# Which engine adds the second row of a pair: by tile, or by what stands beside the pair

## The chip, the cores and the metric

The kernel runs on one core of a Trainium2 chip. The metric is the device time of one execution in microseconds (us). A core has TensorE (PE in the profile; its weight loads are PEld), VectorE (DVE), ScalarE (ACT), GpSimd (POOL) and SyncE (SP), each with its own queue of instructions, and 16 DMA engines. Here SP issues the ordinary transfers and GpSimd the gathers by index.

## What is computed

One layer of a hybrid encoder for 1024 prompt tokens and 64 sample tokens, with 1024 values each. The first half, here called the front, is a normalization, a projection to 3608 columns, three mixers (a gated linear attention, an attention with forgetting, a cross-attention into 256 memory tokens), a gated mix of their outputs and an output projection. The second half is a retrieval of experts, of which there are 16,384. It is this half that the change touches:

```python
def one_block(xb):                       # 128 tokens
    q = (xb @ w_q).reshape(blk, PEER_HEADS, 2, PEER_DHALF)
    s = jnp.einsum('thpc,hpkc->thpk', q, sub_keys, ...)
    ...                                  # the best 16 experts of a token and head: idx, softmax weights g
    u = jnp.take(u_tab, idx, axis=0)
    a = jax.nn.gelu(jnp.einsum('thkd,td->thk', u, xb, ...), approximate=False)
    w = (g * a).astype(xb.dtype)
    return jnp.einsum('thk,thkd->td', w, jnp.take(v_tab, idx, axis=0))
```

For each token, 8 heads choose 16 experts each. An expert is one row u and one row v of 1024 values; in the kernel the two lie side by side in one row of 8 KB. The output is the sum of the rows v, each weighted by its softmax weight times the gelu of the dot product of u and the token.

## The kernel before

**Tiles and groups.** The 1088 tokens are 9 tiles of 128 (the last has 64). The front works on groups of tiles: tile 0, tiles 1 and 2, tiles 3 to 5, tiles 6 to 8. While the experts of one group's tiles are worked through, the front of the next group runs beside them; the first group's front runs alone, and beside the last group's experts nothing runs.

**Pairs.** The experts are worked through in pairs: for tile i, head r and number q, two expert rows for each of the 128 tokens, 8 pairs for a head and 64 for a tile, 544 in all (the last tile packs its 64 tokens twice and has 32). GpSimd gathers the two rows into two of the 8 slots of `c_ring` (L1847, 128 rows of 8 KB for each). VectorE forms the two dot products (L1768, each a long instruction and a short one that reads the accumulator into `l_dots`). ScalarE takes the gelu (L1448), multiplies with the softmax weights (L1451) and scales a unit matrix with the result (L1456, into `l_diag`). TensorE multiplies this diagonal with the v half of the slot and adds into `c_p_y` in PSUM, two matmuls of 512 columns for a row (L1284; in the trace each of them is two records). The second row can instead be added by VectorE in SBUF: `l_ysb` = row times weight + `l_ysb` (L1784), and then its diagonal isn't built. At a tile's end `finish` adds `c_p_y` and `l_ysb` (L1795). A slot is gathered into again when the pair that used it is done: GpSimd waits for TensorE (`s_vdone`) and, where VectorE adds the second row, for `s_vapart` too. It runs three pairs ahead of VectorE.

**Who adds the second row.** `apart(n)` says for pair n whether VectorE does. Before, it does so for all tiles of the first three groups (384 pairs); for the last group's 160 pairs TensorE adds both rows.

**The order.** `make_plan` writes one list of steps: after each pair stand the steps of the next group's front that belong beside it, spread by weights, and the last 16 pairs of a group have none. The steps are `in_prep` (normalization), `in_unit` (projection), `mix`, `fox` and `past` (the mixers), `gate` (gated mix), `out` (output projection) and `sco` (scores of the experts). Each engine walks this list. TensorE takes the steps beside a pair first and then the pair's matmuls. VectorE takes the pair's dot products, then the second row of the pair before (`values`), then a piece of the choice of experts for a later head (`pick`, L1710 to L1758), and then the steps. ScalarE takes the pair first too.

In the walk that follows, stretches of the trace are named by the front's steps beside which they run. For the last group that is 2254 to 2467 us for the projection, 2467 to 3010 for the mixers, 3010 to 3286 for the gated mix, 3396 to 3516 for the scores, 3516 to 3603 for the tail without steps; from 3603 us on the last group's experts run alone.

Of the kernel before, what the change touches and what calls it, by code (L numbers as in the profile page):

```python
# [74 lines left out]

def pair_index(i, r, q):
    return (i * HEADS + r) * 8 + q if i < TILES else TILES * HEADS * 8 + r * 4 + q


def apart(n):  # L80


    return ALL_PAIRS[n][0] < GROUPS[-1][0]


def apart_before(n):
    return sum(apart(k) for k in range(n))


ALL_PAIRS = [(i, r, q) for i in range(NT) for r in range(HEADS) for q in range(pairs_of(i))]  # L90
# [62 lines left out]
def make_plan():  # L153


    plan = [(None, [s]) for s, _ in front_steps(0)]
    plan.append((("start",), []))
    for g in range(len(GROUPS)):
        pairs = [("pair", i, r, q) for i in GROUPS[g] for r in range(HEADS) for q in range(pairs_of(i))]
        ahead = front_steps(g + 1) if g + 1 < len(GROUPS) else []  # L160
        total = sum(w for _, w in ahead)
        slots = len(pairs) - 2 * pairs_of(GROUPS[g][-1])
        done, k = 0.0, 0
        for n, pair in enumerate(pairs):
            beside = []
            while k < len(ahead) and done + ahead[k][1] / 2 <= total * (n + 1) / slots:
                beside.append(ahead[k][0])
                done += ahead[k][1]
                k += 1
            plan.append((pair, beside))  # L170
        assert k == len(ahead)
    plan.append((("end",), []))
    return plan


class Scope:
# [302 lines left out]
def layer(nc, c, t_in, outs, dram, ctx):  # L479

    m = Scope(nc, ctx, "l")
    sb, pb, sem = m.sb, m.pb, m.sem
    PLAN = make_plan()


    wa2, ba_bc, go_bc, bf_bc, gq_bc, gk_bc, gm_bc = c.wa2, c.ba_bc, c.go_bc, c.bf_bc, c.gq_bc, c.gk_bc, c.gm_bc
# [991 lines left out]
    def _(dve):  # L1478
# [294 lines left out]
        def values(n):  # L1773
# [1 line left out]
                return  # L1775
            i, r, q = ALL_PAIRS[n]
            T, j, col = width_of(i), (n * PAIR + 1) % RING, q * PAIR + 1
            if r == 0 and q == 0:
                dve.wait_ge(s_xres, 16 * (i + 1))
            if n:  # L1780
                dve.wait_ge(s_vapart, apart_before(n))
            dve.wait_ge(s_diag, n + 1)
            y = ysb[i % 2]
# [3 lines left out]
        def finish(i):  # L1787
            T = width_of(i)
            r, q = HEADS - 1, pairs_of(i) - 1
            dve.wait_ge(s_vdone, pair_index(i, r, q) + 1)  # L1790
            dve.wait_ge(s_xres, 16 * (i + 1))
            if apart(pair_index(i, r, q)):
                dve.wait_ge(s_vapart, apart_before(pair_index(i, r, q) + 1))
            y = ysb[i % 2]
            tt(out=y[:T, :], in0=p_y[:T, :], in1=y[:T, :], op=ALU.add).then_inc(s_yev, 1)  # L1795
# [150 lines left out]
```

## Time and profile before

| | |
|---|---|
| median of 3 runs | 4438.22 us (4433.03 to 4452.79) |
| profiled execution | 4445.82 us, span 4444.1 us |
| TensorE busy | 3389.7 us (76%) |
| VectorE busy | 2805.9 us (63%) |
| ScalarE busy | 1582.2 us (36%) |
| GpSimd busy | 1216.8 us (27%) |
| moved by DMA | 1484.95 MB, mean 334 GB/s |
| granted TensorE clock, mean | 0.875 of full speed |

The busy time of an engine is a sum over stretches that have different limits. The granted clock has two levels, 1.2 and 2.4 GHz; a mean of 0.75 in a stretch says that half of it passed at 1.2 GHz. TensorE's matmuls are pipelined and their ends are modelled, so its busy time overstates its work. Where the chain of waits names an instruction, that instruction ended last at that point; the same instruction elsewhere may cost nothing.

### The profile page before, as it was taken

Reading aid. Unit: us, or ns where it says so; the run is one execution under the profiler, and the core shown is the slowest. Engines: PE = TensorE matmul, PEld = TensorE weight load, DVE = VectorE, ACT = ScalarE, POOL = GpSimd, SP = SyncE. Lnnn points to the kernel's source line nnn. Section 1 sums busy time; section 2 is a strip of 40 time slices with the busy share of each in tenths; the row PEclk is TensorE's granted clock in tenths of the full one; section 3 lists DMA queues with packets and bytes.
Section 4 is the critical chain, followed back from the end, with each engine's and each line's share of the span. In section 5 each row is a group of like instructions: output and inputs, shape, how many; then the busy total and the mean of one; then the engine's idle time right before and its main releaser. Section 6 shows DMA issues by size and latency. Waiting matters only on the chain.

```text
span 4444.1 us, 33979 instructions
## 1 busy us (share of the span) xinstructions
PE 3389.7 (76%) x10219; PEld 1759.7 (40%) x10219; DVE 2805.9 (63%) x6048; ACT 1582.2 (36%) x3679; POOL 1216.8 (27%) x1122
## 2 busy tenths in 40 slices
PE   5765965986896776989689777576978867777777
PEld 4462444842444443544234344233543322322222
DVE  1112454547656784646777788685767886676677
ACT  1111154422315563432232455253443233333333
POOL 0000211113221222322333232242323344444443
PEclk9787976997997788999889778778989989999989
DMA  7557865889996788879999897878989999999998
GB/s 239 189 200 270 333 215 196 321 319 387 364 351 238 257 306 325 339 291 352 402 387 422 310 362 283 295 285 356 413 351 370 403 414 421 418 415 421 402 373 371
DMA packets 298492, 1484.95 MB, mean 334 GB/s; under 512 B 42740, under 2 KB 112372, under 8 KB 147716
## 3 DMA queue, kind: packets, MB, share of 16 engines
q0 software_dynamic: 156672, 1140.92, 64.7%
q1 hardware_dynamic: 141636, 341.86, 21.2%
q8 instruction: 81, 1.33, 0.1%
q14 instruction: 103, 0.84, 0.0%
HBM read 1415.59 MB, written 67.08 MB: 334 GB/s over the span
## 4 chain that ended last, share of the span: by engine, by line
PE 40%; DMA 24%; DVE 18%; ACT 6%; issue 6%; POOL 2%; SPq 1%; POOLq 0%; DVEq 0%; ACTq 0%
DMA c_ring<-in_uv,l_idx 17%; PE c_p_y L1284 11%; DVE c_ring L1768 7%; PE c_PB L1016 4%; PE c_PC L1016 4%; DVE l_ysb L1784 3%; PE c_PA L1271 2%; PE c_PA L1226 2%; PE c_PB L1271 2%; PE c_PB L1226 2%; PE c_PC L1226 2%; DMA c_area<-oT_sp 2%; POOL c_ring L1847 2%; PE c_PA L1254 1%; DMA c_area<-in_w_out 1%
## 5 line engine op out<-in xcount | busy, mean ns | idle before, releaser
L1847 POOL DMA_INDIRECT c_ring<-in_uv,l_idx x1088 | 1210.0, 1112 | 3203.8 <-PE c_p_y L1284 1400.0
L1284 PE MATMUL c_p_y<-c_ring,l_diag 128*128 128x512 f32 (+1 forms) x2816 | 1510.5, 676 | 451.5 <-ACT l_diag L1456 444.3
L1768 DVE CUSTOM_DVE_ANT_0 c_ring<-c_ring,l_h_cur 128x1024 f32<-128x1024 f32 x1088 | 1302.8, 1221 | 365.1 <-DMA c_ring<-in_uv,l_idx 356.6
L1284 PEld LDWEIGHTS c_p_y<-c_ring,l_diag 128*128 128x128 f32 (+1 forms) x2816 | 551.0, 207 | 1237.6 <-ACT l_diag L1456 650.9
L1448 ACT ACTIVATE l_gel<-l_dots 128x2 f32<-128x2 f32 x544 | 110.7, 203 | 1606.2 <-DVE l_dots L1768 1604.9
L1784 DVE SCALAR_TENSOR_TENSOR l_ysb<-c_ring,l_wgt,l_ysb 128x1024 f32<-128x1024 f32 x384 | 492.4, 1282 | 0.0
L1448 ACT ACT_TABLE_LOAD x207 | 265.6, 1283 | 60.0 <-DVE l_dots L1768 56.6
L1451 ACT ACTIVATE l_wgt<-l_gel,l_gw 128x1 f32<-128x1 f32 x1088 | 261.2, 287 | 17.9
L1456 ACT ACTIVATE l_diag<-c_ident,l_wgt 128x128 f32<-128x128 f32 x640 | 243.1, 399 | 16.7
L1016 PE MATMUL c_PB<-c_area 128*128 128x451 f32 (+1 forms) x576 | 228.4, 550 | 1.9 <-ACT c_area L1317 1.2
L1016 PE MATMUL c_PC<-c_area 128*128 128x451 f32 (+1 forms) x576 | 226.4, 546 | 4.3 <-DMA c_area<-in_w_in 4.3
L1226 PE MATMUL c_PA<-c_area 128*128 128x128 f32 (+3 forms) x512 | 132.1, 415 | 115.8 <-DMA c_area<-oT_sp 113.5
L1016 PEld LDWEIGHTS c_PB<-c_area 128*128 128x128 f32 (+1 forms) x576 | 107.1, 187 | 122.8 <-issue 119.0
L1226 PEld LDWEIGHTS c_PA<-c_area 128*128 128x128 f32 x512 | 93.5, 203 | 155.2 <-issue 126.0
L1016 PEld LDWEIGHTS c_PC<-c_area 128*128 128x128 f32 (+1 forms) x576 | 105.9, 185 | 123.7 <-issue 117.2
L1668 DVE TENSOR_TENSOR c_area<-c_area,c_PA 128x128 f32<-128x128 f32 (+3 forms) x32 | 14.0, 438 | 205.8 <-ACT c_area L1405 205.8
L1166 PE MATMUL c_PC<-c_ident,c_area 128*128 128x128 f32 (+2 forms) x328 | 66.4, 318 | 98.7 <-ACT c_area L1392 54.2
L1271 PE MATMUL c_PA<-c_area 128*128 128x512 f32 (+1 forms) x288 | 130.3, 607 | 1.9 <-ACT c_area L1414 1.9
L1271 PE MATMUL c_PB<-c_area 128*128 128x512 f32 (+1 forms) x288 | 128.3, 599 | 2.5 <-DMA c_area<-rw_sp 2.5
L1226 PE MATMUL c_PB<-c_area 128*128 128x128 f32 (+3 forms) x512 | 123.8, 395 | 0.0
L1226 PE MATMUL c_PC<-c_area 128*128 128x128 f32 (+3 forms) x512 | 122.9, 393 | 0.0
L1254 PE MATMUL c_PA<-c_area 128*128 128x512 f32 (+1 forms) x192 | 91.3, 632 | 24.9 <-DMA c_area<-in_w_out 21.8
(284 smaller groups left out, 3679.4 us busy)
## 6 DMA issues: line engine op xcount, KB each, us to landing
c_area<-in_w_gb SPq DMA_DIRECT2D x32, 2304.0 KB, 10.0
c_area<-in_w_in SPq DMA_DIRECT2D x32, 1804.0 KB, 9.2
c_area<-rw_sp SPq DMA_DIRECT2D x16, 2048.0 KB, 10.8
c_ring<-in_uv,l_idx POOLq DMA_INDIRECT x1088, 10.1
c_area<-in_w_out SPq DMA_DIRECT2D x8, 2048.0 KB, 9.7
proj<-c_area SPq DMA_DIRECT2D x64, 225.5 KB, 7.1
c_area<-proj SPq DMA_DIRECT2D x8, 1288.0 KB, 6.0
c_ring<-in_w_qT SPq DMA_DIRECT2D x16, 512.0 KB, 7.6
```

The costliest lines, as they stand in the source:

```text
L1016: ins = mm_(banks[2 + u % 4][:T, :PW], hT_in[:, dt, j * 128:j * 128 + T], w[:, dt * PW:(dt + 1) * PW], start=dt == 0, stop=dt == DT - 1)
L1166: ins = tr_(PC[:widths[b], (b % 4) * 128:(b % 4) * 128 + T], prob[h % 2][:T, b * 128:b * 128 + widths[b]], c.ident[:T, :T])
L1226: mm_(ps[:, 0:N], w[:, at:at + 128], g_hT[:, e, 0:N], start=e == 0, stop=e == DT - 1)
L1254: ins = mm_((PA, PB)[j % 2][:T, half * 512:(half + 1) * 512], mixT[:, dt, j * 128:j * 128 + T], w[:, dt * 512:(dt + 1) * 512], start=dt == ...
L1271: ins = mm_(banks[v % 4][:T, :], hT_out[:, dt, j * 128:j * 128 + T], w[:, dt * 512:(dt + 1) * 512], start=dt == 0, stop=dt == DT - 1)
L1284: ins = mm_(p_y[:T, e * 512:(e + 1) * 512], diag[:, j, :T], ring[:, j, D + e * 512:D + (e + 1) * 512], start=r == 0 and q == 0 and k == 0, ...
L1448: a_(gel[:, c0:c0 + PAIR], dots[:, c0:c0 + PAIR], ACT.Gelu).then_inc(s_ae, 1)
L1451: ins = nc.scalar.mul(wgt[:, c0 + k:c0 + k + 1], gel[:, c0 + k:c0 + k + 1], gw[:, head % 3, c0 + k:c0 + k + 1])
L1456: ins = nc.scalar.mul(diag[:, (n * PAIR + k) % RING, :T], unit[:, :T], wgt[:, c0 + k:c0 + k + 1])
L1768: ins = nc.vector.tensor_tensor_reduce(out=ring[:, j, 0:D], in0=ring[:, j, 0:D], in1=h_cur[i % 2][:, :], scale=1.0, scalar=0.0, op0=ALU.mu ...
L1784: nc.vector.scalar_tensor_tensor(out=y[:T, :], in0=ring[:T, j, D:2 * D], scalar=wgt[:T, col:col + 1], in1=y[:T, :], op0=ALU.mult, op1=ALU. ...
L1847: nc.gpsimd.indirect_dma_start(out=ring[:, j, :], out_offset=None, in_=t_in["uv"][:, :], in_offset=bass.IndirectOffsetOnAxis(ap=idx[:, hea ...
```

## The change

Whether VectorE adds a pair's second row no longer goes by the pair's tile but by what stands beside the pair in the plan: it does so where one of the steps is `in_unit`, `gate`, `out` or `sco`. Beside mixer steps alone, beside `in_prep` alone, and where no step stands, TensorE adds both rows. For this the plan is made once, ahead of the functions that ask. `values` and `finish` count the rows that VectorE has added so far instead of taking every pair before.

```diff
-def apart(n):
-    return ALL_PAIRS[n][0] < GROUPS[-1][0]
-
-def apart_before(n):
-    return sum(apart(k) for k in range(n))
...
+PLAN = make_plan()
+
+def sums_apart():
+    return [any(step[0] in ("in_unit", "gate", "out", "sco") for step in beside)
+            for expert, beside in PLAN if expert and expert[0] == "pair"]
+
+APART = sums_apart()
+
+def apart(n):
+    return APART[n]
+
+def apart_before(n):
+    return sum(APART[:n])
...
-            if r == 0 and q == 0:
-                dve.wait_ge(s_xres, 16 * (i + 1))
-            if n:
+            dve.wait_ge(s_xres, 16 * (i + 1))
+            if apart_before(n):
                 dve.wait_ge(s_vapart, apart_before(n))
...
-            if apart(pair_index(i, r, q)):
+            if apart_before(pair_index(i, r, q) + 1):
                 dve.wait_ge(s_vapart, apart_before(pair_index(i, r, q) + 1))
```

By the plan 168 pairs keep their second row on VectorE. The 216 others are these:

| the front of group | beside mixers | no step, scattered | no step, tail | `in_prep` |
|---|---|---|---|---|
| tiles 1, 2 | 12 | 0 | 16 | 1 |
| tiles 3 to 5 | 36 | 8 (6 in the gated mix, 1 in the output projection, 1 in the scores) | 16 | 2 |
| tiles 6 to 8 | 67 | 39 (11 in the projection, 1 after the mixers, 14 in the gated mix, 5 in the output projection, 8 in the scores) | 16 | 3 |

Three places show what moves. The line numbers after the change are 10 higher. First VectorE before, beside the forgetting attention of tile 7, two pairs with the steps behind them (L1648 copies transposed probabilities, L1641 and L1642 mask scores and take their maximum):

```order
L1768 ISA c_ring,l_dots<-c_ring,l_h_cur 128x1024
L1768 ISA l_dots 128x1
L1768 ISA c_ring,l_dots<-c_ring,l_h_cur 128x1024
L1768 ISA l_dots 128x1
L1784 SCALAR_TENSOR_TENSOR l_ysb<-c_ring,l_wgt,l_ysb 128x1024
L1641 TENSOR_TENSOR c_PB<-c_PB,c_causal 128x128
L1642 TENSOR_REDUCE l_fmax<-c_PB 128x1
L1648 COPY c_area<-c_PC 128x384
```

And the same place on VectorE after the change:

```order
L1778 ISA c_ring,l_dots<-c_ring,l_h_cur 128x1024
L1778 ISA l_dots 128x1
L1778 ISA c_ring,l_dots<-c_ring,l_h_cur 128x1024
L1778 ISA l_dots 128x1
L1651 TENSOR_TENSOR c_PB<-c_PB,c_causal 128x128
L1652 TENSOR_REDUCE l_fmax<-c_PB 128x1
L1658 COPY c_area<-c_PC 128x384
```

The addition into `l_ysb` is gone from between the dot products and the mixer's steps; nothing else moved. TensorE before, in the same attention (L1166 transposes probabilities, L1148 to L1151 form scores, L1179 multiplies with the values):

```order
L1166 MATMUL c_PC<-c_ident,c_area 128x128 x4
L1148 MATMUL c_PB<-c_area 128x512
L1150 MATMUL c_PB<-c_area 128x256
L1151 MATMUL c_PB<-c_area 128x128
L1166 MATMUL c_PC<-c_ident,c_area 128x128 x3
L1179 MATMUL c_PC<-l_V,c_area 128x64 x7
L1284 MATMUL c_p_y<-c_ring,l_diag 128x512 x2
```

And TensorE there after the change:

```order
L1176 MATMUL c_PC<-c_ident,c_area 128x128 x4
L1158 MATMUL c_PB<-c_area 128x512
L1160 MATMUL c_PB<-c_area 128x256
L1161 MATMUL c_PB<-c_area 128x128
L1176 MATMUL c_PC<-c_ident,c_area 128x128 x3
L1189 MATMUL c_PC<-l_V,c_area 128x64 x7
L1294 MATMUL c_p_y<-c_ring,l_diag 128x512 x4
```

The pair's matmuls have become four, at the same point, ahead of the next step's transposes. Last, TensorE before in the projection of the last group (L1016), where every third pair or so has no step:

```order
L1016 MATMUL c_PB<-c_area 128x451 x8
L1284 MATMUL c_p_y<-c_ring,l_diag 128x512 x4
L1016 MATMUL c_PB<-c_area 128x451 x8
L1284 MATMUL c_p_y<-c_ring,l_diag 128x512 x2
L1016 MATMUL c_PC<-c_area 64x451 x8
```

And TensorE there after the change:

```order
L1026 MATMUL c_PB<-c_area 128x451 x8
L1294 MATMUL c_p_y<-c_ring,l_diag 128x512 x6
L1026 MATMUL c_PB<-c_area 128x451 x8
L1294 MATMUL c_p_y<-c_ring,l_diag 128x512 x2
L1026 MATMUL c_PC<-c_area 64x451 x8
```

Where a pair with a step and one without follow each other, four matmuls have become six: the pair without a step brings two more between two units of the projection.

## Rows read from the trace of the kernel before

**Rows 1.** The page: busy time, and the chain that ended last, by engine

```profile
PE 3389.7 (76%) x10219; PEld 1759.7 (40%) x10219; DVE 2805.9 (63%) x6048; ACT 1582.2 (36%) x3679; POOL 1216.8 (27%) x1122
...
PE 40%; DMA 24%; DVE 18%; ACT 6%; issue 6%; POOL 2%; SPq 1%; POOLq 0%; DVEq 0%; ACTq 0%
```

**Rows 2.** Windows by stretch; the first row names the columns

```profile
core 0: us, PE busy (x) PEld busy (x) DVE busy (x) ACT busy (x) POOL busy (x), PEclk, DMA share, GB/s
...
572.00:727.00 155.00, 106.51 (x478) 76.26 (x478) 98.01 (x211) 88.50 (x178) 23.29 (x23) 0.72 0.52 181
...
1017.00:1118.00 101.00, 61.69 (x100) 21.72 (x99) 75.38 (x155) 23.79 (x73) 36.32 (x32) 0.76 0.98 389
...
1321.00:1665.00 344.00, 251.34 (x1052) 159.29 (x1051) 255.71 (x546) 203.93 (x386) 72.08 (x73) 0.77 0.73 268
1665.00:1935.00 270.00, 235.47 (x689) 131.06 (x688) 161.37 (x328) 111.88 (x205) 71.06 (x61) 0.94 0.85 329
...
2254.00:2467.00 213.00, 206.99 (x505) 89.50 (x504) 168.22 (x336) 56.46 (x171) 79.84 (x70) 0.97 1.01 415
2467.00:3010.00 543.00, 372.96 (x1359) 207.46 (x1358) 417.65 (x879) 263.06 (x541) 160.92 (x137) 0.75 0.83 305
...
3396.00:3516.00 120.00, 115.54 (x260) 46.35 (x259) 92.42 (x180) 30.81 (x94) 45.62 (x40) 0.98 0.99 397
3516.00:3603.00 87.00, 49.44 (x76) 16.14 (x75) 75.28 (x154) 23.30 (x72) 37.76 (x32) 0.80 1.00 404
3603.00:4264.00 661.00, 487.22 (x1022) 189.78 (x1023) 461.57 (x1126) 226.82 (x709) 275.94 (x259) 0.97 1.01 416
```

**Rows 3.** Windows of the forgetting attention: tile 5, then tiles 6, 7, 8

```profile
1590.00:1665.00 75.00, 64.51 (x313) 42.23 (x314) 66.49 (x139) 52.82 (x99) 18.54 (x19) 0.86 0.81 300
2541.00:2631.00 90.00, 72.96 (x296) 44.95 (x295) 81.75 (x165) 51.20 (x101) 28.91 (x28) 0.83 0.96 358
2691.00:2782.00 91.00, 73.30 (x274) 43.66 (x273) 80.08 (x154) 54.93 (x102) 26.75 (x24) 0.81 0.76 275
2892.00:2985.00 93.00, 72.15 (x234) 33.21 (x235) 79.85 (x176) 53.49 (x110) 38.72 (x25) 0.73 0.75 281
```

**Rows 4.** The chain by line in the three mixer stretches, 572:727, 1321:1665, 2467:3010

```profile
by line: DVE c_ring L1768 11.4%; PE c_p_y L1284 5.7%; issue 4.9%; PE c_PC L1166 4.7%; ACT L1392 4.1%; ACT c_area L1392 3.6%; PE c_PC L1099 3.2%; DVE l_ysb L1784 3.1%; ACT c_area L1358 2.5%; PE c_PA L1059 2.5%; PE c_PC L1068 2.4%; PE c_PA L1
...
by line: DVE c_ring L1768 11.9%; issue 8.7%; PE c_p_y L1284 6.9%; DMA c_ring<-in_uv,l_idx 6.1%; DVE l_ysb L1784 5.6%; PE c_PC L1166 3.4%; PE c_PC L1179 3.2%; DMA l_V<-proj 3.1%; PE c_PC L1099 2.0%; PE c_PB L1148 2.0%; ACT c_area L1358 1.7%;
...
by line: DVE c_ring L1768 17.2%; issue 9.6%; DVE l_ysb L1784 8.9%; PE c_p_y L1284 5.5%; DMA c_ring<-in_uv,l_idx 3.5%; DMA l_V<-proj 2.7%; DMA c_area<-in_fox_logf 2.1%; DMA oT_sp<-c_area 2.0%; PE c_PB L1148 1.8%; PE c_PC L1068 1.5%; DMA kT_s
```

**Rows 5.** The chain by line in 2254:2467, 3396:3516, 1665:1935, 3010:3286

```profile
by line: DMA c_ring<-in_uv,l_idx 28.0%; PE c_PB L1016 23.4%; PE c_p_y L1284 17.3%; PE c_PC L1016 11.7%; issue 5.2%; DVE l_ysb L1784 3.4%; DVE c_ring L1768 3.2%; POOL c_ring L1847 2.9%; DVE c_area L1515 0.6%; DVE l_pos L1732 0.5%; ACT l_wgt 
...
by line: DMA c_ring<-in_uv,l_idx 34.8%; PE c_PA L1271 23.7%; PE c_p_y L1284 15.6%; PE c_PB L1271 11.6%; issue 5.5%; POOL c_ring L1847 4.8%; DVE l_ysb L1784 2.0%; DVE c_ring L1768 1.4%; DVE l_onehot L1743 0.6%; DVE l_isel L1745 0.6%; DVE l_o
...
by line: PE c_p_y L1284 18.4%; PE c_PA L1226 16.0%; PE c_PB L1226 15.3%; PE c_PC L1226 14.7%; PE c_PA L1229 7.6%; PE c_PB L1229 7.6%; DMA c_area<-oT_sp 7.0%; PE c_PC L1229 6.7%; DMA oT_sp<-c_area 4.5%; issue 0.7%; DVE c_ring L1768 0.4%; SPq
...
by line: DMA c_ring<-in_uv,l_idx 15.5%; issue 12.0%; DVE c_ring L1768 11.3%; DMA c_area<-in_w_out 9.4%; DMA c_area<-oT_sp 8.3%; DVE l_ysb L1784 6.5%; DMA oT_sp<-c_area 4.0%; ACT L1405 3.3%; PE c_PB L1226 3.2%; PE c_p_y L1284 3.2%; PE c_PC L
```

**Rows 6.** The page's groups: VectorE's row and ScalarE's diagonal

```profile
L1784 DVE SCALAR_TENSOR_TENSOR l_ysb<-c_ring,l_wgt,l_ysb 128x1024 f32<-128x1024 f32 x384 | 492.4, 1282 | 0.0
...
L1456 ACT ACTIVATE l_diag<-c_ident,l_wgt 128x128 f32<-128x128 f32 x640 | 243.1, 399 | 16.7
```

**Rows 7.** Pieces of the chain: start us, us, what; four records are one row

```profile
1477.59 1.72 PE c_p_y L1284 x4
...
2531.13 3.66 PE c_p_y L1284 x4
...
3625.18 3.71 PE c_p_y L1284 x8
```

**Rows 8.** Waits in 2467:3010, then in 1321:1665: us in total, times, longest

```profile
POOL c_ring L1847 <- DVE l_ysb L1784: 335.1, 58, 23.8
...
POOL c_ring L1847 <- DVE l_ysb L1784: 205.0, 27, 18.7
```

More of the change, by code:

```diff
@@ L482, in layer @@
     sb, pb, sem = m.sb, m.pb, m.sem
-    PLAN = make_plan()
     wa2, ba_bc, go_bc, bf_bc, gq_bc, gk_bc, gm_bc = c.wa2, c.ba_bc, c.go_bc, c.bf_bc, c.gq_bc, c.gk_bc, c.gm_bc
```

## The prediction

> **What bounds the kernel now.** I read the page first, then the table of windows by stretch, then the chain of waits inside the stretches, then who waits for whom. On the page no engine is full: TensorE is busy for 76% of the span, and the chain that ended last is TensorE for 40%, DMA for 24% and VectorE for 18% [rows 1]. Such shares average over stretches with different limits, so the table of windows is the view that decides [rows 2]. Three kinds of stretch show in it.
>
> Beside the mixers (572 to 727, 1321 to 1665 and 2467 to 3010 us, together 1042 us) no resource is full: DMA share 0.52, 0.73 and 0.83, and a granted TensorE clock of 0.72 to 0.77, so TensorE spends about half of that time at 1.2 GHz instead of 2.4. VectorE is nearest to full, above all in the attention part: 81.75 of 90 us, 80.08 of 91, 79.85 of 93, 66.49 of 75 [rows 3].
>
> Beside projection, gated mix and scores TensorE is close to full: 206.99 of 213 us in the last group's projection, 115.54 of 120 in its scores, 235.47 of 270 in the gated mix of the third group [rows 2]. In the first two of these the DMA engines are full as well (shares 1.01 and 0.99).
>
> In the tails of a group, and in the whole last stage from 3603 us, DMA is full (0.98 to 1.01) [rows 2].
>
> The profiled execution took 4445.8 us with a span of 4444.1; the median of the runs is 4438.2. The sum below is a difference against the profiled execution; I apply it to the median, which is 7.6 us lower.
>
> **What changes.** Of 384 pairs whose second row VectorE adds, 168 keep this and 216 go to TensorE. Each of the 216 loses one VectorE instruction of 1.28 us on average (277 us in all) and gains a second diagonal on ScalarE, 0.40 us (86 us), and two more matmuls [rows 6]. A row on TensorE has three prices in the chain: 1.72 us at 2.4 GHz, 3.66 us at 1.2 GHz, and 3.71 us for two rows in the last stage [rows 7]. At 1.72 us the 216 rows are 372 us of TensorE. So the change moves more work than it takes away, and what counts is where. The 216 are 115 pairs beside mixer steps, 48 in the tails (16 each), 47 pairs without a step of their own, scattered among the steps of the third and the last group, and 6 beside the preparation steps. No DMA is added or moved, and the queues of SP and GpSimd keep their order. The wait that `values` now makes for the residual at every pair is long fulfilled after the first pair of a tile, so I count it at nothing.
>
> **Beside the mixers (115 pairs).** The three stretches are those of the second, the third and the last group of tiles. I take the terms from the chain of waits [rows 4].
> 1. VectorE's row leaves the chain: 3.1% of 155 us, 5.6% of 344 and 8.9% of 543 are 4.8 + 19.3 + 48.3 = 72 us. Gain 72.
> 2. TensorE's row is on the chain for 5.7%, 6.9% and 5.5% of the same stretches: 8.8 + 23.7 + 29.9 = 62 us. It doubles. With half the time at 1.2 GHz a row now costs about 1.72 x 1.5 = 2.58 us. What the clock will be no row of the mixers shows; the nearest are the tails and the last stage, the same loop of pairs with one row on TensorE (granted 0.76 and 0.80) and with two (0.97) [rows 2]. More work in the gaps should lift the mixers' clock too, though their gaps come from other waits. I take 0.9, nearer to the last stage than to now. Two rows then cost 2 x 1.72 x 1.2 = 4.13 us, 1.6 times one row now. Loss 37. The bounds are 21 (clock full, 3.44 against 2.58) and 62 (clock as now).
> 3. The other TensorE steps on the chain get faster with the clock. The named ones are 12.8%, 10.6% and 3.3% of the three stretches, 74 us, and the lines cut off hold more. By 1.2 / 1.5 the named ones give 15 us; I take 25. Bounds 0 and 45.
> 4. ScalarE's second diagonal: 115 x 0.40 = 46 us of an engine that is busy for half the stretch; a quarter of it on the chain. Loss 12.
> 5. Where VectorE was last by less than a row of TensorE, TensorE comes last instead. About 60 places (72 us by 1.20) can turn; a quarter of them by about 1 us. Loss 15. Bounds 8 and 30.
> 6. GpSimd's gathers waited for VectorE's row at 58 places for 335 us in the last mixer stretch, at 27 for 205 in the one before [rows 8]. That row stands in VectorE's queue behind the dot products of the next pair, while TensorE's stands right behind its own pair's steps, so a slot comes free some 2 us earlier. The chain holds 6.1% and 3.5% of ring transfers there, 40 us; I take a third. Gain 12.
>
> The sum is -72 + 37 - 25 + 12 + 15 - 12 = -45 us. A second reading agrees: in the attention stretches VectorE falls by 1.28 us a pair, but in the first part of the last group (2541 to 2631 us) the DMA share is already 0.96, so nearly nothing is left there, and the others can give some 10 us each [rows 3].
>
> What the Trainium skill says bears on step 2. In "TensorE: Matmul & The Clock Gate", section "What's actually happening", it says that "the default state is throttled, and activity releases the throttle". The tails and the last stage agree with it (0.76 and 0.80 against 0.97). By that rule alone the mixers would go to the last stage's clock; that is the second rival.
>
> **Pairs without a step, among TensorE's own steps (47).** Here the change adds to the engine that is late. In the last projection 11 pairs bring 18.9 us; TensorE's lines are 52.4% of the chain there, so 9.9, less 2.3 us of VectorE's row: +8. In the last scores 8 pairs bring 13.8 us at 50.9%, so 7.0, and since 115.54 + 13.8 is over 120 I take +8. In the third group's gated mix 6 pairs bring 10.3 us at 86.3%: +9. In the last gated mix 14 pairs bring 24 us, but the chain there is DMA and VectorE, with TensorE's named lines at 6.4% and VectorE's row at 6.5%: 0, between -5 and +10 [rows 5]. The other 8, and the 6 beside preparation: 14 x 1.72 us, a quarter on the path, +6. Together +31, between +18 and +45.
>
> **Tails (48 pairs).** VectorE's row leaves the chain, but DMA has a share of 0.98 to 1.00 there. The last stage, with two rows on TensorE, makes a pair in 661 / 128 = 5.17 us; the third tail makes one in 87 / 16 = 5.44 and the first in 101 / 16 = 6.3, with loads for the next group in between [rows 2]. I take -6 for the three, between -15 and +2.
>
> **The sum.** -45 + 31 - 6 = -20 us, from the median of 4438 to 4418 us.
>
> **Rivals.**
> *TensorE becomes the bound (slower).* The mixers' clock stays where it is, because the gaps there are waits for VectorE and ScalarE that a second row doesn't fill. Then step 2 costs 62, step 3 gives nothing, step 5 costs 30: -72 + 62 + 12 + 30 - 12 = +20. With the scattered pairs at +40 and the tails at -2 that is +58: 4496 us. It decides from a granted clock of about 0.8 in the mixers downwards. For it speaks that TensorE's idle time there is in waits, against it the last stage.
> *The clock rises as in the last stage (much faster).* Step 2 costs 21, step 3 gives 45, step 5 costs 8: -72 + 21 - 45 + 12 + 8 - 12 = -88; with +31 and -6 that is -63: 4375 us. For it speaks 0.97 with two rows a pair; against it that a mixer's pair takes 8 to 13 us, not 5.2, with longer gaps.
> *The transfers hide it (no change).* Once VectorE is quicker, the rings run into the DMA engines, as in the attention stretch with a share of 0.96; the mixers give only 15 us, and 31 are lost: +10, 4448 us. For it speaks the share of 0.83 over the last mixer stretch; against it 0.75 and 0.76 in two of its three attention parts.
> That the change doesn't do what it says is excluded by the instructions in order.
>
> **How the numbers follow.** The forecast (-20, between -45 and +5) has 0.38, the full clock 0.24, the transfers 0.18, TensorE as the bound 0.20. A measurement of this kernel tells about 0.5%, 22 us, from no change. Faster by more than that: just over half of the forecast (0.21) and all of the full clock: 0.45. Slower: nearly all of the last case (0.19) and a little of the transfers: 0.22. The rest is 0.33. The range reaches down past the full clock with the better bounds of the other terms (-88 us, 4350) and up to +27 (4465), which leaves out the worse half of the slower case. The likeliest case's own range is 4393 to 4443.
>
> **What would show it.** Right: in the attention stretches VectorE is no longer busy for 0.86 or more of the time; the granted clock of the three mixer stretches is near 0.9; the last projection and the last scores are each some 8 us longer; the tails are hardly shorter; GpSimd waits for TensorE's row in the mixers. Wrong: mixer stretches that are longer than before or at an unchanged clock (then TensorE's row takes the share of the chain that VectorE's had), or that shrink by over 80 us; and scattered pairs that cost nothing, because the DMA engines hid them.

## The result, and the profile after

The changed kernel took 4466.61 us (median of 7 runs, 4456.53 to 4477.17), the kernel before 4444.09 (7 runs): a ratio of 1.0049, interval [1.0033, 1.0064], so 15 to 28 us slower where 20 us faster was forecast. The profiled execution took 4461.3 us with a span of 4459.6.

The page of the changed kernel, busy time and chain by engine:

```profile
PE 3616.6 (81%) x11083; PEld 1871.8 (42%) x11083; DVE 2551.0 (57%) x5832; ACT 1647.1 (37%) x3895; POOL 1214.8 (27%) x1122
...
PE 56%; DMA 22%; DVE 8%; ACT 7%; issue 3%; POOL 1%; SPq 1%; POOLq 0%; DVEq 0%; ACTq 0%
```

Against [rows 1] VectorE lost 255 us of work and went from 18% to 8% of the chain; TensorE went from 40% to 56%. The work moved as planned, and the time did not fall.

Windows by stretch, with the columns of [rows 2]: the three mixer stretches are the rows from 565, 1322 and 2474; tails from 1019 and 3529, third group's gated mix from 1666, last projection from 2255, last scores from 3406:

```profile
core 0: us, PE busy (x) PEld busy (x) DVE busy (x) ACT busy (x) POOL busy (x), PEclk, DMA share, GB/s
565.00:728.00 163.00, 120.39 (x522) 80.54 (x520) 85.34 (x200) 92.61 (x191) 23.90 (x24) 0.79 0.49 172
1019.00:1118.00 99.00, 78.99 (x160) 31.68 (x158) 58.28 (x140) 28.46 (x89) 37.24 (x33) 0.91 0.99 397
1322.00:1666.00 344.00, 282.62 (x1187) 171.30 (x1186) 213.78 (x509) 214.27 (x421) 73.47 (x74) 0.88 0.74 270
1666.00:1943.00 277.00, 245.88 (x711) 135.42 (x710) 153.09 (x320) 112.55 (x208) 74.97 (x59) 0.94 0.83 317
2255.00:2474.00 219.00, 218.63 (x546) 96.43 (x547) 155.08 (x326) 62.37 (x185) 80.46 (x69) 1.00 1.00 402
2474.00:3012.00 538.00, 432.99 (x1630) 237.00 (x1629) 338.43 (x812) 283.76 (x608) 148.77 (x136) 0.88 0.84 307
3406.00:3529.00 123.00, 123.00 (x286) 50.95 (x285) 81.55 (x169) 32.98 (x101) 43.90 (x38) 1.00 0.97 386
3529.00:3618.00 89.00, 71.37 (x147) 27.38 (x145) 57.96 (x139) 28.31 (x89) 37.65 (x35) 0.94 1.00 403
```

Against [rows 2] the mixers take 163, 344 and 538 us instead of 155, 344 and 543: 3 us more in all, where 45 less were forecast. The granted clock there rose from 0.72, 0.77 and 0.75 to 0.79, 0.88 and 0.88: close to the forecast 0.9 in the second and third stretch, not in the first. Timed from the first dot product of its first pair to that of the next stretch, the last projection went from 213.3 to 218.5 us, the last scores from 119.7 to 123.3, the third group's gated mix from 270.0 to 277.0, and the three tails from 286.2 to 284.1 together. The last gated mix, behind the third mixer stretch, went from 275.8 to 282.3 us, so that the two together did not get shorter (818.8 before, 820.3 after). That goes with the mixers' pairs and not with the scattered ones: 281.6 us with only the former moved, 274.6 with only the latter.

The forgetting attention of tiles 5 to 8, same columns:

```profile
1584.00:1666.00 82.00, 74.40 (x349) 46.01 (x350) 54.66 (x129) 56.17 (x108) 18.24 (x20) 0.96 0.75 276
2547.00:2636.00 89.00, 84.47 (x344) 49.50 (x343) 65.12 (x150) 55.63 (x115) 26.35 (x27) 0.96 0.93 351
2700.00:2792.00 92.00, 86.54 (x354) 51.56 (x352) 64.32 (x139) 57.94 (x118) 29.30 (x28) 0.94 0.86 310
2918.00:2998.00 80.00, 74.72 (x266) 34.90 (x265) 56.43 (x133) 51.96 (x114) 30.69 (x25) 0.94 0.89 334
```

VectorE fell from 0.86 or more to about 0.7 in all four [rows 3], but only the last (80 us for 93) is shorter; tile 5 is longer (82 for 75), the others are unchanged.

The chain by line in the three mixer stretches of the changed kernel (first, second, third):

```profile
by line: PE c_p_y L1294 15.6%; DVE c_ring L1778 7.7%; PE c_PC L1176 4.7%; ACT L1402 4.7%; ACT c_area L1402 3.8%; PE c_PC L1078 3.0%; issue 2.8%; PE c_PC L1189 2.6%; PE c_PC L1109 2.4%; ACT c_area L1368 2.4%; PE c_PA L1069 2.3%; ACT l_diag L
...
by line: PE c_p_y L1294 23.5%; DVE c_ring L1778 8.0%; PE c_PC L1189 4.9%; PE c_PC L1176 3.8%; issue 3.7%; DMA l_V<-proj 3.1%; DVE l_fmax L1652 2.6%; ACT l_diag L1466 2.3%; PE c_PB L1158 2.3%; ACT L1458 2.2%; PE c_PC L1109 1.9%; ACT l_wgt L1
...
by line: PE c_p_y L1294 27.3%; DVE c_ring L1778 8.1%; DMA c_area<-in_fox_logf 4.5%; DMA oT_sp<-c_area 4.0%; PE c_PC L1189 3.5%; DMA c_ring<-in_uv,l_idx 3.2%; DMA l_V<-proj 2.7%; PE c_PC L1176 2.6%; issue 2.5%; ACT l_diag L1466 2.5%; DVE l_f
```

TensorE's rows (line 1294) are 15.6%, 23.5% and 27.3%, 253 us, where they were 62 [rows 4]. Counted as pieces of the chain, they stand there 61 times, and 22 times before. VectorE's row is no longer among the lines shown, and the dots (line 1778) fell from 152 to 84 us. The chain in the last projection and the last scores:

```profile
by line: PE c_p_y L1294 36.8%; PE c_PB L1026 33.5%; PE c_PC L1026 29.6%; ACT l_diag L1466 0.3%; issue 0.0%
...
by line: PE c_p_y L1294 39.1%; PE c_PA L1281 33.7%; PE c_PB L1281 28.0%
```

Nothing but TensorE is left there (the pairs' rows, the projection's and scores' matmuls), where transfers were the first line before [rows 5].

### The profile page after: what moved, and what is told of

Same layout as the page of the kernel before. It is cut to its first block, busy times and chain, and to the rows that moved or that the text cites. A ratio compares the mean times of both kernels' runs of the same rounds, so it can differ in the third digit from the quotient of the medians.

```text
span 4459.6 us, 35301 instructions
## 1 busy us (share of the span) xinstructions
PE 3616.6 (81%) x11083; PEld 1871.8 (42%) x11083; DVE 2551.0 (57%) x5832; ACT 1647.1 (37%) x3895; POOL 1214.8 (27%) x1122
## 4 chain that ended last, share of the span: by engine, by line
PE 56%; DMA 22%; DVE 8%; ACT 7%; issue 3%; POOL 1%; SPq 1%; POOLq 0%; DVEq 0%; ACTq 0%
PE c_p_y L1294 20%; DMA c_ring<-in_uv,l_idx 14%; PE c_PB L1026 5%; PE c_PC L1026 5%; DVE c_ring L1778 4%; PE c_PB L1281 3%; PE c_PA L1236 3%; PE c_PA L1281 3%; PE c_PC L1236 3%; PE c_PB L1236 3%; DMA c_area<-oT_sp 2%; ACT l_diag L1466 1%; POOL c_ring L1856 1%; PE c_PA L1239 1%; PE c_PC L1239 1%
## 5 line engine op out<-in xcount | busy, mean ns | idle before, releaser
L1294 PE MATMUL c_p_y<-c_ring,l_diag 128*128 128x512 f32 (+1 forms) x3680 | 1794.7, 632 | 329.5 <-ACT l_diag L1466 327.8
L1294 PEld LDWEIGHTS c_p_y<-c_ring,l_diag 128*128 128x128 f32 (+1 forms) x3680 | 700.3, 198 | 1289.8 <-issue 775.7
L1466 ACT ACTIVATE l_diag<-c_ident,l_wgt 128x128 f32<-128x128 f32 x856 | 306.1, 395 | 16.7
L1793 DVE SCALAR_TENSOR_TENSOR l_ysb<-c_ring,l_wgt,l_ysb 128x1024 f32<-128x1024 f32 x168 | 215.7, 1284 | 0.8 <-ACT l_diag L1466 0.8
L1281 PE MATMUL c_PA<-c_area 128*128 128x512 f32 (+1 forms) x288 | 129.4, 604 | 1.3 <-ACT c_area L1424 1.2
L1236 PEld LDWEIGHTS c_PB<-c_area 128*128 128x128 f32 x512 | 87.9, 191 | 37.2 <-issue 8.6
```

The source lines that it names most:

```text
L1236: mm_(ps[:, 0:N], w[:, at:at + 128], g_hT[:, e, 0:N], start=e == 0, stop=e == DT - 1)
L1281: ins = mm_(banks[v % 4][:T, :], hT_out[:, dt, j * 128:j * 128 + T], w[:, dt * 512:(dt + 1) * 512], start=dt == 0, stop=dt == DT - 1)
L1294: ins = mm_(p_y[:T, e * 512:(e + 1) * 512], diag[:, j, :T], ring[:, j, D + e * 512:D + (e + 1) * 512], start=r == 0 and q == 0 and k == 0, ...
L1466: ins = nc.scalar.mul(diag[:, (n * PAIR + k) % RING, :T], unit[:, :T], wgt[:, c0 + k:c0 + k + 1])
L1793: nc.vector.scalar_tensor_tensor(out=y[:T, :], in0=ring[:T, j, D:2 * D], scalar=wgt[:T, col:col + 1], in1=y[:T, :], op0=ALU.mult, op1=ALU. ...
```

## The experiments

All times are set against runs of the kernel before on the same chip (medians 4443.8 to 4447.1); 0.001 is 4.4 us. Where two experiments are subtracted, the bound given is the root of the sum of squares of their half intervals. Such differences sometimes join runs of two chips, each set against its own runs of the kernel before. A letter in an expectation names a theory of the set of runs in which it stands. My theory after the result: the mixers are one chain in which each engine's part is worth much less than its share, and TensorE's second row and ScalarE's second diagonal together cost what VectorE's row was worth. Rivals: the loss lies in the scattered pairs alone; TensorE's row alone is too dear; the diagonal is the culprit.

### Which of the three places loses

Three kernels each move one kind of pair to TensorE, and a fourth every second mixer pair:

```diff
-APART = sums_apart()
+APART = [own_group(n) and not on_tensor(n) for n in range(len(ALL_PAIRS))]
+def on_tensor(n): return mixers(n)               # 115 pairs
+def on_tensor(n): return bare(n)                 # the 47 scattered ones
+def on_tensor(n): return tail(n) or prep(n)      # 48 + 6
+def on_tensor(n): return mixers(n) and n % 2 == 0
```

> One part of the change alone: TensorE adds both rows for the 115 pairs beside mixer steps; the 47 scattered pairs without a step, the 48 tail pairs and the 6 beside preparation keep VectorE's row. Theory A (beside the mixers TensorE becomes the engine that ends last, so its row costs what VectorE's gave): between -8 and +10 us against before, 4436 to 4454. Theory B (the mixers do gain the forecast's 45 us and the other pairs lose it all and more): about -45 us, 4400.

> One part of the change alone: TensorE adds both rows only for the 47 scattered pairs without a step of their own. Theory A (the loss of the whole change is these pairs, beside steps in which TensorE ends last): +15 to +25 us, 4459 to 4469. Theory B (they cost more than the whole change, since the mixers gain): +50 us or more. A third reading, that DMA hides them: within 5 us of before.

> One part of the change alone: TensorE adds both rows for the 48 pairs in the groups' tails and the 6 beside preparation. Both theories: between -8 and +2 us, since the DMA engines are full in the tails (the two traces differ by -2 us there).

> Beside the mixers TensorE adds both rows for every second pair only (58 of 115); all other pairs as before. Theory A (before, VectorE ends last there, after the change TensorE does, and the best lies between): -10 to -30 us against before, 4414 to 4434. If each moved row has the same price wherever it is, half of the result for all 115: between -4 and +5 us.

Measured: mixers alone 0.9990 [0.9977, 1.0002], -4 us; scattered pairs alone 1.0046 [1.0030, 1.0063], +20 us; tails and preparation 0.9989 [0.9976, 1.0003], -5 us; every second mixer pair 1.0009 [0.9996, 1.0022], +4 us. The scattered pairs alone lose as much as the whole change, and the mixers give nothing. The first three came out as theory A had it; sharing the mixers' rows between the engines gives nothing either, a miss of its theory A and within the other reading (between -4 and +5). The parts add to +11 and the whole is +22; with about 6 us of doubt on each part that is not a contradiction. Two later runs point at where the 11 us may lie: with the mixers and the tails on TensorE already, moving the scattered pairs too costs 31 us (1.0034 less 0.9965, plus or minus 8; both with the two signals of the section after next), where alone it costs 20 (plus or minus 7). The two prices are not told apart for certain, so whether the moves hinder each other stays open.

### What the mixers' row is worth on each engine

Beside the mixers alone, four kernels take the parts apart; all other pairs are as before:

```diff
# neither engine adds the second row; one diagonal       (left out of the sum)
# as that, and ScalarE builds the second diagonal        (left out of the sum)
# TensorE adds both rows, both with the first's diagonal (not the reference's weights)
+diag[:, (n * PAIR) % RING if mixers(n) else j, :T]
# VectorE and TensorE both add it                        (counted twice)
```

> Left out: beside the mixers (115 pairs) the second row is added by no engine, and its diagonal isn't built; all other pairs as before. Theory A (the row is on the path with either engine, at about the same price): it gains what VectorE's row had on the chain, 50 to 75 us against before, 4370 to 4395; TensorE's row then has given nearly all of that back. Theory C (VectorE's row was not worth its share of the chain, since another wait ends right behind it): 0 to -20 us, 4424 to 4444.

> Left out: beside the mixers no engine adds the second row, but ScalarE builds its diagonal. Against the run in which it isn't built this is the price of the diagonal alone. The forecast's term: +12 us. Theory D (ScalarE's in-order diagonal is what eats the gain): +35 us or more, up to its whole 46 us. Theory A: 5 to 15 us.

> Changed: beside the mixers TensorE adds both rows, but multiplies the second with the first one's diagonal, so that ScalarE builds one (the second row gets the wrong weight). Against the run with all 115 pairs on TensorE (4443) this is the price of the diagonal with TensorE's row in place: theory A +0 to -15 us, 4428 to 4443; theory D -35 to -46 us. Against the run without any second row it is the price of TensorE's row: theory A 45 to 65 us.

> Doubled: beside the mixers both engines add the second row (it is counted twice in the output); all other pairs as before. Against before this adds TensorE's row and ScalarE's second diagonal and takes nothing away. Theory A (engines end last in turn, so that costs add): +40 to +70 us, 4484 to 4514. Theory C (waits of the mixers hide either row): 0 to +20 us.

Measured: neither 0.9861 [0.9841, 0.9882], -62 us; diagonal alone 0.9895 [0.9877, 0.9912], -47; TensorE's row alone 0.9934 [0.9915, 0.9953], -29; both engines 1.0077 [1.0061, 1.0092], +34.

The first is in theory A's range and the second at its edge. The other two lie between the ranges: TensorE's row cost less than theory A had, the diagonal beside it more than A and less than D, and both engines' rows together 34 us where A had at least 40.

So VectorE's row costs 62 us when nothing replaces it, not much less than its 72 us of the chain; my theory that every part is worth much less than its share fails there. TensorE's row costs 33 us (0.9934 less 0.9861, plus or minus 12). The diagonal costs 15 without TensorE's row (plus or minus 12), and 25 with it (0.9990 less 0.9934, plus or minus 10). Taken in this order: -62 + 33 + 25 = -4. In the other order, TensorE's row and diagonal on top of VectorE's cost 34, and taking VectorE's away then gives 39, not 62: once TensorE's second row is there, about a third of the price of VectorE's row is gone.

### Why the second diagonal costs that much

Pieces of the chain of the changed kernel in tile 8's attention (start us, us, what):

```profile
2917.90 1.13 DVE c_ring L1778
2919.04 1.14 DVE c_ring L1778
2920.45 0.49 ACT l_wgt L1461 x2
2920.97 0.69 ACT l_diag L1466 x2
2921.68 1.28 ACT L1450
2922.97 0.40 ACT l_ex L1450 x2
2923.37 0.48 ACT c_area L1379
...
2940.54 0.75 DVE l_fmax L1652
2941.29 1.13 DVE c_ring L1778
2942.43 1.14 DVE c_ring L1778
2943.84 0.49 ACT l_wgt L1461 x2
2944.36 0.70 ACT l_diag L1466 x2
2945.10 3.70 PE c_p_y L1294 x8
2948.80 0.39 PE c_PC L1176 x4
2949.19 1.00 PE c_PA L1158 x2
```

Two readings offer themselves. From 2940.54 one turn of the chain: VectorE's maximum, two dots, ScalarE's weights and two diagonals, TensorE's two rows (3.70 us), the next matmuls of the mixer. The diagonal stands ahead of the row. But at 2920.97 it stands ahead of ScalarE's next work (line 1450, the exponential in the choice of experts for a later head, with its table load of 1.28 us), and TensorE does not come into it. In the three mixer stretches the diagonals stand on the chain at 36 places: at 11 TensorE's row follows, at 25 ScalarE's own next step. The experiments ask what that costs. First, one semaphore for each diagonal, so that TensorE starts its first row without the second:

```diff
+                if k == 0: pe.wait_ge(s_diag, n + 1)
+                else:      pe.wait_ge(s_diag2, both_before(n + 1))
-            ins.then_inc(s_diag, 1)          # behind both diagonals
+                ... .then_inc(s_diag2 if k else s_diag, 1)
```

The second kernel adds the tails, the third is the whole change with the two signals; the fourth leaves the second row of the 47 scattered pairs out.

> The 115 pairs beside the mixers on TensorE, as in the run of the mixers alone (0.999 of before), but ScalarE raises a semaphore after each of the two diagonals, so that TensorE's first row starts after the first and the second diagonal is built beside it. Theory A: the second diagonal costs about 25 us there because the first row waits for it too (115 times about 0.4 us is 46 at most, 25 measured); then the whole of it goes and the time is 0.993 to 0.995 of before, 4415 to 4423 us. Rival B: it costs because it holds ScalarE's own steps or because TensorE's row is what decides; then the time stays at 0.998 to 1.000, 4436 to 4445. The last group's pairs keep one signal for both diagonals.

> The same with the 54 pairs of the tails and of the preparation on TensorE as well, and the two signals in the last group too; the 47 scattered pairs stay on VectorE. Theory A: the parts add up: -28 (mixers with two signals) -5 (tails) and something from the last group, 4400 to 4412 us, 0.990 to 0.993 of before, faster than both kernels. Rival B (the signal does nothing): 0.997 to 0.999, 4433 to 4440.

> The whole change with the two signals, in the last group too. Theory A: the change measured 1.005 of before; the two signals take 25 to 40 us from it, so 0.995 to 0.999, 4423 to 4440, and 15 to 25 us slower than the version that leaves the 47 scattered pairs on VectorE. Rival B: 1.003 to 1.005, 4455 to 4466.

> Beside the 47 scattered pairs without a step no engine adds the second row and its diagonal is not built (that row is left out of the sum); all other pairs as before. Theory A: beside these pairs VectorE's row lies beside TensorE and costs nothing, so that TensorE's row is a pure loss: 0.998 to 1.000 of before, 4435 to 4445 us. Rival B: VectorE's row is on the path here too and TensorE's row merely dearer than it: 0.990 to 0.995, 4400 to 4423.

Measured: 0.9978 [0.9967, 0.9989]; with tails 0.9965 [0.9953, 0.9978], 16 us faster than before by the ratio (11 by the medians, 4435.63 against 4447.08) and so faster than both kernels; the whole change with two signals 1.0034 [1.0022, 1.0047]. The signal gives 5 us of the 25 (0.9990 less 0.9978, plus or minus 7, which does not tell it from nothing). All three fit rival B, whose range each interval reaches, and not theory A. The scattered pairs without a second row: 1.0005 [0.9993, 1.0018]. VectorE's row costs nothing there that the runs can tell, theory A, and TensorE's costs the whole 20 us. The chain of the last projection shows why, first with the scattered pairs on TensorE:

```profile
by line: PE c_p_y L1321 37.2%; PE c_PB L1053 33.8%; PE c_PC L1053 29.5%
```

and with their row added by no engine:

```profile
by line: DMA c_ring<-in_uv,l_idx 35.6%; PE c_PB L1053 20.6%; PE c_p_y L1321 15.6%; PE c_PC L1053 11.5%; issue 5.2%; POOL c_ring L1883 3.6%; DVE l_ysb L1820 2.3%; DVE c_ring L1805 2.1%; ACT l_wgt L1488 0.7%; ACT l_diag L1493 0.6%; DVE c_area
```

With TensorE's row the stretch is all TensorE and takes 217.2 us; with no second row the ring's transfers are back as the longest line, and the stretch takes 212.6 us, as before (213.3), so that VectorE's row had cost nothing.

Next, two kernels take the diagonal off ScalarE:

```diff
# GpSimd, behind its own next gather
+pool.wait_ge(s_ae, 2 * n + 2)
+nc.gpsimd.tensor_scalar(out=diag[:, (n * PAIR + 1) % RING, :T], in0=c.ident[:, :T], scalar1=wgt[:, col:col + 1], ...)
# VectorE, behind the next pair's dots; TensorE adds the row behind the next pair's first
+nc.vector.tensor_scalar(out=diag[:, j, :T], in0=c.ident[:, :T], scalar1=wgt[:, col:col + 1], ...)
+if n and not first and behind(n - 1): late()
```

> The 115 pairs beside the mixers on TensorE (0.999 of before), but GpSimd builds the second diagonal, once ScalarE has the pair's weights and behind its own next gather, so that ScalarE builds one. Theory C: the second diagonal costs because it stands between two pieces of ScalarE's own mixer work, not because TensorE waits for it (raising the signal between the two gave only 5 us); then taking it off ScalarE brings the time towards the run with one diagonal and TensorE's row (0.9934): 0.993 to 0.996 of before, 4416 to 4430 us, if GpSimd builds it within about a microsecond. Rival D: what the second row waits for and TensorE's own order decide, whichever engine builds it: 0.998 to 1.003, 4438 to 4460.

> The same pairs, but VectorE builds the second diagonal after the next pair's dots, where it would have added the row, and TensorE adds that row behind the next pair's first row (the last pair of a tile as in the changed kernel). VectorE then writes 128x128 in place of the 128x1024 sum of 1.28 us, ScalarE builds one diagonal, and no row waits in the chain of the pair. Theory C: 0.990 to 0.995, 4400 to 4425 us, at least as good as 0.9934. Rival D: the row stands in TensorE's order behind the next mixer step and gives the ring's slot back as late as VectorE's row did, so 0.997 to 1.003, 4435 to 4460.

Both missed theory C and lost more than rival D's range allows (up to 1.003): GpSimd 1.0055 [1.0037, 1.0072], VectorE 1.0063 [1.0047, 1.0078]. The traces show a different change of the chain in each. The diagonals on ScalarE and on GpSimd (ns: least, median, most):

```profile
L1499 ACT ACTIVATE l_diag<-c_ident,l_wgt x640: 385/402/404, 423.1 to 4282.5; 128x128 f32<-128x128 f32 x160
L1908 POOL TENSOR_SCALAR l_diag<-c_ident,l_wgt x115: 602/625/3372, 572.7 to 3028.2; 128x128 f32<-128x128 f32 x115
```

and the chain of GpSimd's kernel in the third mixer stretch:

```profile
by line: PE c_p_y L1327 29.7%; POOL c_ring L1889 10.8%; POOL l_diag L1908 5.6%; DVE c_ring L1811 4.9%; issue 4.4%; DMA c_area<-in_fox_logf 4.4%; PE c_PC L1220 3.0%; DMA l_V<-proj 2.9%; PE c_PC L1207 1.9%; SPq L891 1.8%; PE c_PB L1189 1.4%; 
```

A diagonal takes 625 ns on GpSimd against 402, and GpSimd, which has 0.9% of the chain of this stretch before, holds 16.4% of these 558 us with its gathers and diagonals. VectorE's diagonal is the quickest of the three:

```profile
L1839 DVE TENSOR_SCALAR l_diag<-c_ident,l_wgt x114: 270/282/313, 589.1 to 3027.8; 128x128 f32<-128x128 f32 x114
```

but the same stretch's chain in its kernel is now

```profile
by line: PE c_p_y L1328 24.9%; DMA c_ring<-in_uv,l_idx 16.7%; DVE c_ring L1827 6.3%; issue 4.1%; DMA c_area<-in_fox_logf 4.0%; PE c_PC L1225 2.8%; POOL c_ring L1914 2.0%; PE c_PC L1212 1.9%; DMA c_area<-in_cache_mem_v 1.8%; DMA l_V<-proj 1.
```

with 16.7% of 555 us in ring transfers (3.5% before [rows 4]). VectorE's dots wait for them (us in total, times, longest):

```profile
DVE c_ring L1827 <- DMA c_ring<-in_uv,l_idx: 49.4, 40, 2.8
```

In the run of the mixers alone that was 4.8 us, 6 times. The row that TensorE adds a pair later gives its slot back later, and the gathers come late. So neither run tells whether ScalarE's time was the cause. The next one does: TensorE's rows as in the run with one diagonal, and ScalarE builds the second for no reader. With it went a try of TensorE's row in the third mixer stretch only (67 pairs, and the tails and the preparation):

```diff
             ins.then_inc(s_diag, 1)
+            if mixers(n):
+                nc.scalar.mul(diag[:, (n * PAIR + 1) % RING, :T], unit[:, :T], wgt[:, c0 + 1:c0 + 2])
# the other kernel
+def on_tensor(n): return (mixers(n) and n >= 230) or tail(n) or prep(n)
```

> As the run with TensorE's row and one diagonal beside the mixers (second row with the first's diagonal, 0.9934), but ScalarE builds the second diagonal after all, behind the signal, and nothing reads it. Theory C (the diagonal costs by holding ScalarE's own mixer work): 0.9970 to 0.9990, 4430 to 4440 us, as the run with two signals measured (0.9978). Rival D (it costs because TensorE's second row waits for it): 0.9925 to 0.9945, 4411 to 4420 us. The second row is not the reference's.

> Two signals; of the mixers' pairs only the 68 of the third group on TensorE, and the 54 pairs of the tails and the preparation; the rest as before. By the stretches of the profiles TensorE's row took 15 us off the third group's mixers (543 to 528) but put 6 to 7 on the first group's and 1 to 9 on the second's; the tails gave 5. Theory A (the stretches are independent): -15 -5 = -20 us, 0.994 to 0.997 of before, 4417 to 4431 us, faster than both kernels and than the version with all mixers (0.9965). Rival B (the stretches' differences are noise of single profiles): 0.997 to 1.000.

Measured: 0.9979 [0.9966, 0.9991], against 0.9934 [0.9915, 0.9953] without it: 20 us (plus or minus 10) for 115 diagonals that nobody reads. Theory C holds in so far as the diagonal costs through ScalarE and not through TensorE's wait for it. The third mixer stretch without and with it (same columns as the windows above), first without:

```profile
2459.00:2984.00 525.00, 421.94 (x1617) 232.90 (x1616) 339.07 (x813) 263.88 (x541) 147.98 (x136) 0.89 0.85 314
```

and with:

```profile
2461.00:2994.00 533.00, 431.65 (x1624) 236.53 (x1624) 339.22 (x813) 283.72 (x608) 152.19 (x138) 0.87 0.84 308
```

ScalarE is busy for 20 us more and the stretch is 8 us longer (the three together 12, from 1027 to 1039). ScalarE is busy only half of the time, and still its time counts where its next work on the chain queues behind the diagonal. Two such places in the chain of that run, the unread diagonal (line 1496) ahead of a mixer's copy and ahead of the exponential in the choice of experts:

```profile
2862.84 0.29 ACT l_diag L1496
2863.13 0.95 ACT c_area L1370
...
2905.02 0.29 ACT l_diag L1496
2905.32 1.28 ACT L1477
```

It is on the chain at 23 places of the three stretches, 6.8 us together, each time ahead of ScalarE's own next instruction: 17 mixer steps and 6 exponentials of the choice. So not only the mixers' work is held up, and 6.8 of the 20 us (plus or minus 10) are seen directly; the trace does not place the rest. The last kernel measured 0.9973 [0.9960, 0.9985], just beyond theory A's range and just inside rival B's, so it decides between neither; it is not told from the version with all mixers and tails (0.9965). The second group's mixers took 343.7 us before and 350.2 and 352.9 in the two kernels that change only the scattered pairs, so differences of some 9 us between single profiles mean nothing and could not carry this choice. The 8 us between the two profiles above are no larger; there the times of the runs carry the finding.

## Why the prediction was wrong, point by point

The step that failed is **"Beside the mixers (115 pairs)"**, forecast at -45 us and measured at -4 (plus or minus 6). The largest miss in it is the gain from taking VectorE's row off the chain: 84 us forecast with the earlier slots, 62 measured. By its own numbers:

- **1 and 6, VectorE's row and the slots that come free earlier** (72 + 12 forecast). Both together gave 62 (plus or minus 9). That VectorE's row was 72 us of the chain was no price: when it goes, a path that was second takes over after part of it. In the run with no second row that is TensorE's first row: it goes from 62 to 112 us of the chain (stretches of 154, 331 and 500 us)

```profile
by line: DVE c_ring L1805 9.6%; PE c_p_y L1321 8.4%; PE c_PC L1203 4.9%; ACT c_area L1429 4.0%; DVE l_fmax L1679 3.5%; PE c_PC L1136 3.4%; issue 3.4%; PE c_PC L1105 2.5%; ACT c_area L1395 2.5%; PE c_PC L1216 2.5%; ACT L1429 2.5%; PE c_PA L1
...
by line: PE c_p_y L1321 14.3%; DVE c_ring L1805 9.0%; PE c_PC L1216 5.4%; PE c_PC L1203 4.1%; issue 3.9%; DMA l_V<-proj 3.4%; DVE l_fmax L1679 2.9%; DMA c_ring<-in_uv,l_idx 2.5%; PE c_PB L1185 2.5%; PE c_PC L1136 2.3%; ACT L1485 1.9%; ACT c
...
by line: DVE c_ring L1805 14.6%; PE c_p_y L1321 10.4%; DMA c_ring<-in_uv,l_idx 5.4%; DMA c_area<-in_fox_logf 4.9%; DVE l_fmax L1679 4.1%; DMA oT_sp<-c_area 3.8%; issue 3.0%; DMA l_V<-proj 2.8%; ACT l_wgt L1488 2.0%; PE c_PC L1203 1.9%; ACT 
```

 The earlier release is not to be seen: the changed kernel's GpSimd waits for TensorE's row (third mixer stretch, then second; us in total, times, longest)

```profile
POOL c_ring L1856 <- PE c_p_y L1294: 363.1, 67, 21.7
...
POOL c_ring L1856 <- PE c_p_y L1294: 261.5, 37, 19.3
```

 where it waited 335.1 and 205.0 us for VectorE's [rows 8] and another 23.1 and 56.5 for TensorE's, 358 and 262 together. TensorE's second row gives the slot back about as late as VectorE's did. Shortfall 22 us.
- **2, 3 and 5, TensorE's row, its faster other steps, its coming last** (+37 - 25 + 15 = +27). Measured +33 together (plus or minus 12), so the sum was not wrong as far as the runs tell; the clock rose about as assumed. The terms do not fit the chain: TensorE's rows took 253 us of it, where I had counted on 62 + 37 + 15. They stand there at 39 more places (61 less 22), where I had counted on 15. That this cost only 33 us says that most of what stood there before, the dots above all, now lies beside them; which of the three terms is off by how much no run separates. Shortfall 6 us.
- **4, ScalarE's second diagonal** (+12, a quarter of 46 us). Measured 25 (plus or minus 10), half of it. I priced it by the busy share of ScalarE; 20 us (plus or minus 10) come even if nobody reads the diagonal, from what queues behind it on ScalarE. Shortfall 13 us.

These are the 41 us between -45 and -4. Only the first shortfall is far outside the noise. The groups of the page show that the work itself was as counted, 0.40 us a diagonal and 168 rows left to VectorE:

```profile
L1466 ACT ACTIVATE l_diag<-c_ident,l_wgt 128x128 f32<-128x128 f32 x856 | 306.1, 395 | 16.7
...
L1793 DVE SCALAR_TENSOR_TENSOR l_ysb<-c_ring,l_wgt,l_ysb 128x1024 f32<-128x1024 f32 x168 | 215.7, 1284 | 0.8 <-ACT l_diag L1466 0.8
```

- **The second reading**, by VectorE's 1.28 us a pair, failed with the first: in four attention stretches VectorE got free, and three did not get shorter.
- **Scattered pairs** (+31): right in sign, and nearly right that VectorE's row was free, which the forecast had at 2.3 us in the projection. Measured +20 alone and +31 with the other pairs moved, not told apart. In the profile of the whole change the projection (+8 forecast) is 5 us longer, the scores (+8) 4 and the third group's gated mix (+9) 7, all smaller than forecast.
- **Tails** (-6): measured -5 with the preparation, not told from nothing. (661 / 128 is 5.16, not 5.17; nothing hangs on it.)
- **Rivals.** The clock rose (second rival), without its gain: with 0.88 after 0.75 and 0.77 the mixers took as long as before. The sentence quoted from the Trainium skill ("TensorE: Matmul & The Clock Gate", section "What's actually happening") agrees with this rise. The slower rival had the right end, TensorE as the bound, with the wrong condition: it was to decide at a clock of about 0.8 or less, and TensorE came last at 0.88. The transfers (third rival) did not fill up in the mixer stretches: their shares of 0.49, 0.74 and 0.84 are about those of before. The 6 us by which the gated mix behind them grew were not traced to a wait.
- **What would show it**: VectorE's share, GpSimd's waits, the tails and the clock of two of the three mixer stretches came as listed under right; the projection and the scores grew by less than the 8 us listed. What came of the list under wrong is the line that mattered: TensorE's row has the share of the chain that VectorE's had, and more.

## What to carry to other kernels

A step's share of the chain of waits is not its price (72 us of the chain gave 62, with the earlier slots), and what replaces it has to be paid on the same chain: here -62, +33 and +25. In this chain through four engines a short instruction on a half-idle engine counted for about half its time (20 to 25 us of 46, plus or minus 10), whether anyone read its result or not, since that engine's own next steps queue behind it. Where TensorE is the last to end, as in the last projection, VectorE's sum was free (1.0005 without it): leave it there. The version with mixers and tails moved, scattered pairs not, and a signal for each diagonal has the lowest ratio of the kernels that compute the layer, 0.9965 [0.9953, 0.9978], though it is not told from the two nearest (0.9973 and 0.9978).

## What the runs showed that was not expected

- The same 128x128 product of the identity and a column of weights took a median of 282 ns on VectorE, 402 on ScalarE and 625 on GpSimd.
- More work on TensorE raised its granted clock in the mixers by 0.07 to 0.13 of full speed (2.4 GHz), and the three stretches together took 3 us more.
- Adding a row on TensorE one pair later put 16.7% of the chain of a 555 us stretch into the ring's transfers, 3.5% before: with 8 slots there was little to spare there.
